# One of three weight sums per panel moved from VectorE to GpSimd in a transformer block in float32

## The reference

```python
xn = rms_norm(h, norm_mix_g[l])
proj = xn @ w_in[l]
...
merged = jax.nn.sigmoid(g_a) * (o_a @ w_branch_a[l]) + jax.nn.sigmoid(g_b) * (o_b @ w_branch_b[l])
h = h + merged @ w_out[l]
hn = rms_norm(h, norm_ffn_g[l])
h = h + (jax.nn.silu(hn @ w_ffn_gate[l]) * (hn @ w_ffn_up[l])) @ w_ffn_down[l]
```

## Time and profile before

| | us |
|---|---|
| median of 3 runs (1304.59 to 1304.71) | 1304.65 |
| the profiled execution | 1304.68 |
| its span in the trace | 1302.9 |
| TensorE busy | 1283.1 (98%) |
| VectorE busy | 967.0 (74%) |
| ScalarE busy | 706.1 (54%) |
| GpSimd busy | 65.0 (5%) |

### The profile page before, as it was taken

How to read it: one execution, slowest core, us unless ns; L and a number is a source line. 1 busy time by engine, 2 the same in 40 slices (tenths; PEclk the granted TensorE clock), 3 DMA queues, 4 the chain that set the end, 5 groups by cost and what they waited for, 6 DMA issues and landing times.

```text
span 1302.9 us, 15236 instructions
## 1 busy us (share of the span) xinstructions
PE 1283.1 (98%) x5956; PEld 1055.3 (81%) x5956; DVE 967.0 (74%) x935; ACT 706.1 (54%) x755; POOL 65.0 (5%) x65
## 2 busy tenths in 40 slices
PE   7999999999999999999999999999999999999998
PEld 6888887777788888888788888888888888888877
DVE  6555556777555554667898988787898988798986
ACT  5444444666544444455556655555566555565553
POOL 1112110000000000000100000000000000000000
PEclk9999999999999999999999999999999999999999
DMA  8565556454475555665866696887856698866864
GB/s 259 197 201 187 193 189 190 152 153 152 136 256 189 192 193 194 204 248 178 242 249 202 196 290 218 240 236 243 282 203 213 207 274 260 252 209 206 284 198 125
DMA packets 135442, 276.53 MB, mean 212 GB/s; under 512 B 5121, under 2 KB 11329, under 8 KB 132945
## 3 DMA queue, kind: packets, MB, share of 16 engines
q1 hardware_dynamic: 129344, 250.37, 56.2%
q0 software_dynamic: 6032, 25.26, 10.2%
HBM read 249.38 MB, written 8.41 MB: 198 GB/s over the span
## 4 chain that ended last, share of the span: by engine, by line
PE 96%; DVE 2%; issue 1%; ACT 1%; DMA 0%; SPq 0%; ACTq 0%; DVEq 0%
PE bank L1559 18%; PE bank L1561 17%; PE bank L1560 17%; PE bank L1515 13%; PE bank L1517 13%; PE bank L1516 13%; PE bank L1463 1%; PE bank L1448 1%; PE bank L1473 1%; PE bank L1488 1%; PE bank L1591 1%; DVE staged L1072 0%; DMA x_rows<-in_x 0%; DVE xT_lo L1081 0%; DVE w_lo L1063 0%
## 5 line engine op out<-in xcount | busy, mean ns | idle before, releaser
L1265 DVE TENSOR_TENSOR u_lo<-quad,u_hi 128x2048 fp32r<-128x2048 f32 x187 | 424.0, 2286 | 80.2 <-ACT u_hi L923 43.3
L923 ACT ACTIVATE u_hi<-quad 128x2048 fp32r<-128x2048 f32 x187 | 355.0, 1914 | 214.6 <-PE bank L1561 119.5
L1063 DVE TENSOR_TENSOR w_lo<-raw,w_hi 128x1024 fp32r<-128x1024 f32 (+1 forms) x192 | 229.1, 1201 | 196.1 <-ACT w_hi L777 194.4
L777 ACT ACTIVATE w_hi<-raw 128x1024 fp32r<-128x1024 f32 (+1 forms) x192 | 199.1, 1041 | 257.6 <-PE bank L1517 255.8
L1515 PE MATMUL bank<-w_hi,xT_hi 128*128 128x512 f32 (+1 forms) x544 | 214.0, 393 | 3.9 <-DVE w_lo L1063 2.5
L1517 PE MATMUL bank<-w_lo,xT_hi 128*128 128x512 f32 (+1 forms) x544 | 209.3, 385 | 0.0
L1516 PE MATMUL bank<-w_hi,xT_lo 128*128 128x512 f32 (+1 forms) x544 | 209.1, 384 | 0.0
L1559 PE MATMUL bank<-u_hi,xT_hi 128*128 128x512 f32 x484 | 188.7, 390 | 3.4 <-issue 1.8
L1561 PE MATMUL bank<-u_lo,xT_hi 128*128 128x512 f32 x484 | 188.3, 389 | 0.0
L1560 PE MATMUL bank<-u_hi,xT_lo 128*128 128x512 f32 x484 | 188.3, 389 | 0.0
L1515 PEld LDWEIGHTS bank<-w_hi,xT_hi 128*128 128x128 f32 x544 | 102.8, 189 | 26.1 <-issue 2.5
(11 more groups left out here) (170 smaller groups left out, 1574.8 us busy)
## 6 DMA issues: line engine op xcount, KB each, us to landing
raw<-in_w_in SPq DMA_DIRECT2D x64, 1024.0 KB, 5.3
quad<-in_w_ffn_gate SPq DMA_DIRECT2D x44, 1024.0 KB, 6.5
quad<-in_w_ffn_up SPq DMA_DIRECT2D x44, 1024.0 KB, 6.0
quad<-in_w_ffn_down SPq DMA_DIRECT2D x44, 1024.0 KB, 6.3
quad<-quad POOLq DMA_DIRECT2D x17, 1024.0 KB, 8.1
raw<-in_w_out SPq DMA_DIRECT2D x12, 1024.0 KB, 5.0
raw<-in_w_branch_a SPq DMA_DIRECT2D x8, 1024.0 KB, 5.0
raw<-in_w_branch_b SPq DMA_DIRECT2D x8, 1024.0 KB, 5.0
```

What stands on the lines that cost most here:

```text
L777: A(w_hi[:, p % SPLIT_SLOTS, 0:w], raw[:, c % RAW_SLOTS, (p % 2) * w:(p % 2 + 1) * w], ACT.Copy).then_inc(hi_ready, 1)
L923: A(u_hi[u.hi][:], quad[slot][:], ACT.Copy).then_inc(hi_ready, 1)
L1063: V.tensor_tensor(w_lo[:, p % SPLIT_SLOTS, 0:w], raw[:, p // 2 % RAW_SLOTS, (p % 2) * w:(p % 2 + 1) * w], w_hi[:, p % SPLIT_SLOTS, 0:w].bi ...
L1265: V.tensor_tensor(u_lo[u.lo][:], quad[u.panel.slot[u.raw]][:], u_hi[u.hi][:].bitcast(F32), ALU.subtract).then_inc(lo_ready, 1)
```

## The change

Z is made by GpSimd. It waits there for R (`sum_ready`, now two per panel) and for M2's low part, and counts a semaphore of its own, `z_ready`, on which ScalarE waits ahead of M4 and SyncE ahead of the load. In GpSimd's queue it stands behind Q and the first output transfer and ahead of the second; in panel 0 it stands ahead of the store of h. It is GpSimd's first elementwise operation on a full weight tile.

```diff
+        z_ready = sem("z_ready")
...
-            return {"P": 3 * panel.n + 1, "R": 3 * panel.n + 2, "Z": 3 * panel.n + 3}[name]
+            return {"P": 2 * panel.n + 1, "R": 2 * panel.n + 2}[name]
...
                 elif freed[0] == "sum":
-                    sp.wait_ge(sum_ready, sums(freed[1], "Z"))
+                    sp.wait_ge(z_ready, freed[1].n + 1)
...
+            def sum_z(panel):
+
+                pool.wait_ge(sum_ready, sums(panel, "R"))
+                pool.wait_ge(lo_ready, panel.unit["M2"].index + 1)
+                dst = quad[panel.slot["21"]][:]
+                nc.gpsimd.tensor_tensor(dst, dst, quad[panel.slot["11"]][:], ALU.add).then_inc(z_ready, 1)
+
             for panel in panels:
                 sum_q(panel)
+                if panel.prev is not None and panel.prev.kind == "down":
+                    add_out(panel.prev, 0)
+                sum_z(panel)
                 if panel.n == 0:
                     store_h(NB - 1)
                     pool.wait_ge(h_sum_ready, 1)
                     rsqrt(h_rs[:], h_ms[:], h_sum[:], D, T, h_rs_ready)
                     pool.wait_ge(h_stored, 16 * NB)
                 if panel.prev is not None and panel.prev.kind == "down":
-                    add_out(panel.prev, 0)
                     add_out(panel.prev, 1)
...
-                if u.name in ("M5", "M6", "M4"):
-                    act.wait_ge(sum_ready, sums(panel, {"M5": "P", "M6": "R", "M4": "Z"}[u.name]))
+                if u.name in ("M5", "M6"):
+                    act.wait_ge(sum_ready, sums(panel, {"M5": "P", "M6": "R"}[u.name]))
+                elif u.name == "M4":
+                    act.wait_ge(z_ready, panel.n + 1)
...
-            def sum_z(panel):
-                dst = quad[panel.slot["21"]][:]
-                V.tensor_tensor(dst, dst, quad[panel.slot["11"]][:], ALU.add).then_inc(sum_ready, 1)
-
...
-                if u.name == "N1":
-                    sum_z(panel)
...
-                if u.name == "M2":
-                    sum_z(panel)
-                    if gu:
-                        hidden(before, 0)
+                if u.name == "M2" and gu:
+                    hidden(before, 0)
```

## The result

| | before | changed |
|---|---|---|
| median of 4 runs each, us | 1304.64 (1304.59 to 1304.71) | 1319.67 (1318.88 to 1321.16) |
| the profiled execution, us | 1304.68 | 1318.94 |
| its span, us | 1302.9 | 1317.1 |

The change makes the kernel slower: ratio 1.0116, with a 95% interval of 1.0103 to 1.0128. The forecast was 1318.5 us, in a range of 1303 to 1326.

What follows compares the result with a forecast made beforehand. TensorE was taken as the bound, busy 41.70 of 41.70 us per panel. Terms 6.57+1.05+0.98+0.20+2.46+3.63-1.02 = +13.9 us on 1304.68 gave 1318.6, say 1318.5 us; range 1303 to 1326.

Steps and rivals of the forecast that it cites:

- rival without a stop: All panels: GpSimd's Z doesn't stop VectorE, only panel 0's saving of 1.0 us stays, 1303.6 us; chance 0.17.
- Z's length: Each 128x2048 Z addition on GpSimd: 4.6 us, priced from the 128x128 affine select's whole time per element.
- panel 0, low part held: Panel 0: Z holds M7's low part to 622.43 us, so the last additions to h come 3.63 us late.
- panel 1, early M4: Panel 0's Z done early brings M4's copy forward; TensorE's late start of panel 1's M1 goes, -1.02 us.
- panel 1, product: Panel 1, second product of gate by up: late beyond its 0.28 us margin despite 1.4 gained, 0.20 us.
- panels 3, 9, 15: TensorE stalls ahead of the transposes, 2.19 us each: product 1.90 late plus 1.04 carried in, minus 0.75 margin.
- panel 7: Product 1.90 us late against a margin of 0.85, nothing carried in: 1.05 us.
- panel 13: Like panel 7, product 1.90 us late against a margin of 0.92: 0.98 us.
- panel 16, the wait: Panel 16: Z runs until 1279.56 us and delays M7, whose seed was already just in time: 2.46 us.
- Costed at nothing: M4's copy, the load into Z's freed slot, output additions, the store of h, one more semaphore: no cost expected.
- six quiet panels: Panels 4, 5, 6, 10, 11, 12: M7's low part is held but fits the margins, nothing lost there.

Runs made afterwards that it cites:

- memset kernel: Changed kernel with each Z replaced by three GpSimd memsets of the same 128x2048 tile, written but not read: 1303.46 us, ratio 0.9991.
- one-operand kernel: Changed kernel with Z replaced by a GpSimd multiplication by 1 of the same tile, one operand read: 1304.28 us, ratio 0.9996.
- panel 16 alone: Against the kernel before, only panel 16's Z on GpSimd, the other 16 on VectorE: median 1308.43 us, in two groups, ratio 1.0027.
- a moved line: Kernel before with panel 0's Z, still on VectorE, moved from behind N1 to behind the additions to h: 1303.41 us, ratio 0.9989.
- panel 0 alone: Against the kernel before, only panel 0's Z on GpSimd, the other 16 on VectorE: 1306.88 us, ratio 1.0017.

## Why the prediction was right

**The mechanism.** All of it hung on whether GpSimd's Z stops a low part on VectorE, for which the trace of before had only the other direction. It does: 17 low parts held, each ending about 2.15 us behind Z. The memset kernel excludes that GpSimd's mere activity does it. The rival without a stop would have needed low parts of 2.28 us under a running Z; none is to be seen. What spoke for it, the unlengthened 1.22 us at 34.53 us, could not have told the two apart: a held low part ends about 2.15 us behind GpSimd's instruction, 0.13 less than its own length, so an overlap of 0.16 us hardly shows. In panel 1 of the one-operand kernel the two overlap by 0.13 us, and the low part takes 2.29. The Trainium skill (SBUF — State Buffer, "Who interferes with whom") states that a VectorE instruction with two SBUF inputs contends with a GpSimd one that reads SBUF and not with one that only writes it; both halves agree with the runs here (6.05 and 2.29 us).

**Z's length.** Forecast 4.6, measured 4.60 us. The number was right and its reason was not: it came from a small one-operand row, whose fixed part was to stand in for a second operand. A full tile with one operand takes 1.91 us, not 4.6: for its own kind of work the row would have been off by more than a factor of two. The Trainium skill (GPSIMD Engine Reference, 3.1) gives 4497 ns, 2% under the measured 4604, and was the better ground.

**The terms.** Shifts of the same TensorE work in the two profiled executions, in us:

| place | forecast | measured |
|---|---|---|
| panel 0, low part held | +3.63 | +3.54 |
| panel 1, early M4 | -1.02 | -1.18 |
| panel 1, product | +0.20 | +0.48 |
| panels 3, 9, 15 | +2.19 each | +2.20, +2.21, +2.16 |
| panel 7 | +1.05 | +0.44 |
| panel 13 | +0.98 | +0.18 |
| panel 16, the wait | +2.46 | +2.43 |
| panel 16, the clock | not forecast | +1.59 |
| sum | +13.9 | +14.1 |

The executions differ by 14.3 us; the remainder lies in shifts of under 0.2. Panel 1's product was 0.3 short. In panels 3, 9 and 15 the size was right and the place only in part: the forecast had one wait of about 2.2 us ahead of the transposes, but TensorE starts 0.4 us late already at M1, and loses 1.6 more ahead of the transposes. One reading of the earlier trace rows was off: between the entries of 2.0 and 1.0 us stands one of 1.1, for a seed of e in panel 0; it is there before and after alike and changes nothing in the sum.

**Panels 7 and 13.** These two terms were mis-sized. In panel 7 the low part is held as forecast (4.84 us, to 2.16 behind Z), but TensorE waits less. The margin had been read as fixed, and it isn't: in both panels VectorE's work hangs on a gate product of ScalarE, and that one waits for an output transfer that doesn't move with the rest. ScalarE's waits for it before, changed, with six Z moved (4, 5, 6, 10, 11, 12), and with 2, 3, 8, 9, 14, 15 moved:

```profile
ACT side_a L937 <- DMA out<-evac: 7.5, 2, 3.8
```

```profile
ACT side_a L949 <- DMA out<-evac: 5.9, 2, 3.1
```

```profile
ACT side_a L958 <- DMA out<-evac: 6.4, 2, 3.4
```

```profile
ACT side_a L958 <- DMA out<-evac: 7.5, 2, 3.9
```

Measured against TensorE's work, the transfer landed 0.7 us earlier in panel 7 and 0.9 in panel 13 and gave VectorE that much. It isn't the lateness of the rest that does it: with six Z moved nothing else is late and the waits shrink all the same, from 3.76 to 3.44 us and from 3.70 to 2.98, while with the other six everything is 2 to 4 us late and they stay at 7.5 in sum. So most of it comes from the held low parts of the panels ahead, 4 to 6 and 10 to 12. They free their slots later: in the kernel with six, the load that stands behind panel 5's is issued at 833.08 us instead of 830.98. What in the queues then lets the output transfer land earlier, no run shows.

**Costed at nothing.** The six quiet panels cost 0.2 us together, within what the runs can tell. Nobody waited for Z. Loads were late, though not by Z's own semaphore: behind a down panel the held low part frees its slot 2 us later, and the transfer Q of panels 6, 7, 12 and 13, which had waited for P, now waits for a load and is issued 0.5 to 1 us late against TensorE's work. Nobody waited for Q either.

**The total** is right partly by cancelling: panels 7 and 13 came 1.4 us short, the clock in panel 16 took 1.6 us unforeseen. That the two cancel is luck. The median of the four runs, 1319.67, is 0.7 over the profiled execution. Two of the four took 1318.9, the others 1320.4 and 1321.2. The half clock varies from one execution to the next in the kernel with panel 16 alone, but it doesn't settle this scatter: the slowest of the four has the highest mean clock, 0.999, the other three 0.997. What it is stays open.

## What to carry to other kernels

Before moving an elementwise operation from VectorE to GpSimd, look not at who waits for it but at what VectorE runs meanwhile: in these runs every VectorE instruction with two SBUF operands that met a GpSimd instruction reading SBUF stood until that one was done, which the profile books as busy time of the held instruction. Its price is the hold minus the margin at each place, carried on to the next place as long as VectorE has no idle time, so it has to be followed from place to place. And relief for an engine is worth only the waits that end with it; here all 38.8 us were worth 1.3, which a moved line gave as well.

## What the runs showed of the hardware that was not expected

- TensorE's granted clock fell from 2.4 to 1.2 GHz for about 3.5 us behind a wait of 2.5 us in the changed kernel, at a cost of 1.6 us, and not behind the same wait in the profiled execution of the kernel with panel 16 alone. In panel 0 it fell too: 0.52 and 0.62 in the two stretches of 2 us from 624 us on in the changed kernel, 1.00 in both with panel 0 alone, behind waits of 2.2 us each. There it cost nothing: N0 starts 3.54 us later than before in both kernels, because TensorE at full clock had to wait 1.65 us for N0's low part and at half clock not at all. Behind the waits of up to 1.65 us no drop was seen. A stall of this size on TensorE can so cost more than its length, but not in each execution, and only where nothing else is waited for behind it. The first of the two stretches, changed and with panel 0 alone:

```profile
624.00:626.00 2.00, 1.91 (x9) 1.91 (x10) 0.04 (x1) 1.93 (x5) 0.75 (x1) 0.52 0.99 342
```

```profile
624.00:626.00 2.00, 1.86 (x12) 1.69 (x13) 0.09 (x1) 1.88 (x5) 0.76 (x1) 1.00 0.97 345
```

- GpSimd on 128x2048 float32: 1813 ns to write (memset), 1914 ns with one operand read (scale), 4604 ns with two (addition). The second operand costs more than the rest together.
- The hold is whole: the held low part ends about 2.15 us behind GpSimd's instruction however early it began. Under Z that was 4.28 us for one that began 2.5 us late and 6.46 us for one that began 0.3 us into it.
